# Four ring slots from the output projection to the end of cross-attention, and the first weight quad and y moved in four pieces each

## What is computed

```python
# per layer, x is the residual stream
h = rmsnorm(x, norm_mix); z, xbc, dt, q, k, v, g = split(h @ w_in)
ssd = gated_norm(ssd_scan(silu(causal_conv(xbc)), dt), z)       # 16 heads, new states are outputs
ret = gated_norm(retention(rotary(q), rotary(k), v), g)         # 4 heads, new states are outputs
x = x + concat(ssd, ret) @ w_out
x = x + cross_attend(rmsnorm(x, norm_mem), mem_k, mem_v, w_mq, w_mo)   # 4 heads, 256 memory tokens
x = x + hier_moe(rmsnorm(x, norm_ffn))                          # top group, then top 2 of 16 SwiGLU experts
# after the last layer
y = rmsnorm(x, norm_final)
```

## Time and profile before

| | us |
|---|---|
| median of three runs | 1656.1 (1656.04 to 1657.07) |
| the profiled execution's own time | 1652.09 |
| its span, first to last instruction | 1650.3 |
| TensorE busy (matmul) | 1574.4 (95% of the span) |
| VectorE busy | 548.9 (33%) |
| ScalarE busy | 291.7 (18%) |
| read from memory | 356.42 MB, 231 GB/s with the writes |

### The profile page before, as it was taken

One profiled execution on the slowest core, in us unless ns is written; L12 is line 12 of the kernel. 1 busy time (PEld: TensorE's weight loads), 2 busy tenths in 40 slices (PEclk: granted clock), 3 DMA queues, 4 the chain that ended last, 5 costly groups with the idle time before them and its releaser, 6 DMA issues.

```text
span 1650.3 us, 20355 instructions
## 1 busy us (share of the span) xinstructions
PE 1574.4 (95%) x8720; PEld 996.9 (60%) x8720; DVE 548.9 (33%) x1116; ACT 291.7 (18%) x614; POOL 14.2 (1%) x30
## 2 busy tenths in 40 slices
PE   6999999899998999999999999998999999999996
PEld 4776667677765645445377765685776665444542
DVE  1313754561132411121223066646411314121122
ACT  1003322140111201001100142212311212100102
POOL 0000000000000000000000000000000000000000
PEclk9999999999999999999999999999999999999999
DMA  6324211784257699999713241228733757999990
GB/s 271 134 102 153 87 72 52 294 318 178 103 210 299 248 378 406 394 411 411 299 58 147 102 154 56 71 110 336 276 121 142 295 207 319 409 398 412 405 394 38
DMA packets 28685, 382.48 MB, mean 232 GB/s; under 512 B 3184, under 2 KB 3568, under 8 KB 3888
## 3 DMA queue, kind: packets, MB, share of 16 engines
q1 hardware_dynamic: 25040, 356.43, 54.7%
q0 software_dynamic: 3552, 24.71, 3.7%
HBM read 356.42 MB, written 24.71 MB: 231 GB/s over the span
## 4 chain that ended last, share of the span: by engine, by line
PE 91%; DMA 4%; DVE 2%; ACT 1%; DVEq 1%; issue 1%; SPq 0%; POOL 0%; ACTq 0%; POOLq 0%
PE psum L544 38%; PE psum L1127 13%; PE psum L905 8%; PE psum L1147 7%; PE psum L1172 4%; DMA ring<-stream 4%; PE psum L1102 4%; PE psum L661 1%; PE psum L560 1%; PE psum L551 1%; PE psum L1113 1%; PE psum L984 1%; PE psum L529 1%; PE psum L752 1%; PE psum L1002 1%; PE psum L557 1%
## 5 line engine op out<-in xcount | busy, mean ns | idle before, releaser
L544 PE MATMUL psum<-h,ring 128*128 128x320 f32 x1664 | 460.8, 437 | 3.3 <-DMA ring<-stream 2.5
L544 PEld LDWEIGHTS psum<-h,ring 128*128 128x128 f32 x1664 | 316.9, 192 | 141.7 <-issue 12.0
L1127 PE MATMUL psum<-ring,work 128*64 128x512 f32 x768 | 170.7, 594 | 1.4 <-ACT work L1517 1.4
L905 PE MATMUL psum<-work,ring 128*128 128x320 f32 x512 | 139.7, 433 | 0.9 <-ACT work L1294 0.9
L544 PE MATMUL psum<-mem,ring 128*128 128x256 f32 x512 | 121.4, 393 | 6.4 <-DMA ring<-stream 6.4
L905 PEld LDWEIGHTS psum<-work,ring 128*128 128x128 f32 x512 | 96.5, 190 | 40.7 <-ACT work L1294 1.8
L1127 PEld LDWEIGHTS psum<-ring,work 128*64 128x64 f32 x768 | 53.7, 137 | 108.4 <-issue 106.6
L544 PEld LDWEIGHTS psum<-mem,ring 128*128 128x128 f32 x512 | 98.4, 196 | 27.5 <-DMA ring<-stream 7.3
L1147 PE MATMUL psum<-work 128*64 128x512 f32 x512 | 113.4, 595 | 0.7 <-ACT work L1528 0.7
L544 PE MATMUL psum<-work,ring 128*128 128x320 f32 x256 | 72.1, 444 | 14.1 <-DMA ring<-stream 13.0
L2058 DVE TENSOR_TENSOR x<-x,psum 128x320 f32<-128x320 f32 x128 | 62.5, 488 | 54.9 <-PE psum L1172 49.2
(11 more groups left out here) (284 smaller groups left out, 1369.5 us busy)
## 6 DMA issues: line engine op xcount, KB each, us to landing
ring<-stream SPq DMA_DIRECT2D x120, 2048.0 KB, 9.6
work<-stream SPq DMA_DIRECT2D x32, 2048.0 KB, 9.8
states_out<-stream SPq DMA_DIRECT2D x16, 2048.0 KB, 12.7
st_out<-states_out POOLq DMA_DIRECT2D x12, 1024.0 KB, 11.1
st_out<-work POOLq DMA_DIRECT2D x6, 1024.0 KB, 7.4
mk_out<-k_mem POOLq DMA_DIRECT2D x2, 1024.0 KB, 15.2
mv_out<-work POOLq DMA_DIRECT2D x2, 1024.0 KB, 5.7
x<-x_in SPq DMA_DIRECT2D x1, 1280.0 KB, 5.8
```

The source lines that it names most:

```text
L544: mm = pe.matmul(out, w[:, a:a + P], rhs[:, j, :], start=(j == 0), stop=(j == KD - 1))
L905: mm = pe.matmul(psum[:, j % 4, 0:T], w[:, a:a + P], src, start=(i == 0), stop=(i == 15))
L1127: mm = pe.matmul(psum[ab * CAP:(ab + 1) * CAP, up, :], h_packed[:, p % 2, k, ab * CAP:(ab + 1) * CAP], w[:, a:a + BANK], start=(k == 0), s ...
```

## The change

- `slot_of` gives q20 to q35 four slots in turn, 2, 3, 0, 1, in place of the three of the ring. The experts' six slots are taken in the order 2, 3, 0, 1, 4, 5. `use_of` counts the uses of a slot in a list of all quads.
- The waits ahead of the first load into slot 3 and into slot 4 are bound to those loads: the wait for the state stores stands ahead of q21 (before: q39), that for cross-attention and the memory values ahead of q40 as before.
- x and the parameters are issued ahead of the first constants.
- The very first quad is loaded slab by slab, with a semaphore of its own (`s_slab`) for each of the first three; the first three chunks of the first projection wait for their slab.
- y is stored by SP in four quarters, each once its two chunks are written, in place of two halves by GpSimd.

```diff
--- before.py
+++ after.py
@@ -72,18 +72,20 @@
 XT = 2 + GB
 WIDER = 6
 assert Q_MOE % RING == 0 and (QUADS - Q_MOE) % WIDER == 0
-LATER = (QUADS - Q_MOE) // WIDER
+assert (Q_MOE - Q_OUT) % 4 == 0
 
 
 def slot_of(q):
-    return q % RING if q < Q_MOE else (q - Q_MOE) % WIDER
+    if q < Q_OUT:
+        return q % RING
+    return (2, 3, 0, 1)[(q - Q_OUT) % 4] if q < Q_MOE else (2, 3, 0, 1, 4, 5)[(q - Q_MOE) % WIDER]
+
+
+SLOTS = [slot_of(q) for q in range(QUADS)]
 
 
 def use_of(L, q):
-
-    own = (Q_MOE // RING if slot_of(q) < RING else 0)
-    return L * (own + LATER) + (q // RING if q < Q_MOE else own + (q - Q_MOE) // WIDER)
-
+    return L * SLOTS.count(slot_of(q)) + SLOTS[:q].count(slot_of(q))
 
 
 XW = CW - 1 + SEQ + DB * (CW - 1 + DS)
@@ -295,6 +297,7 @@
 
         loaded = [sem(f"s_loaded{s}") for s in range(WIDER)]
         freed = [sem(f"s_freed{s}") for s in range(WIDER)]
+        s_slab = [sem(f"s_slab{i}") for i in range(3)]
         s_sq = sem("s_sq")
         s_acc = sem("s_acc")
         s_sum = sem("s_sum")
@@ -474,21 +477,27 @@
 
         @block.sync
         def _(sp):
-            sp.dma_start(cst[:, 0:FIRST], consts[:, 0:FIRST]).then_inc(s_const, 16)
             sp.dma_start(x[:], x_in).then_inc(s_const, 16)
             sp.dma_start(par[:], params.rearrange("l p n -> p l n")).then_inc(s_const, 16)
+            sp.dma_start(cst[:, 0:FIRST], consts[:, 0:FIRST]).then_inc(s_const, 16)
             for L in range(DEPTH):
                 for q in range(QUADS):
                     s, n = slot_of(q), use_of(L, q)
                     if n >= 1:
                         sp.wait_ge(freed[s], n)
-                    if q == Q_MOE + RING:
+                    if q == SLOTS.index(3):
                         for i in range(3):
                             sp.wait_ge(s_store[i], 16 * STORES[i] * (L + 1))
-                    if q == Q_MOE + RING + 1:
+                    if q == SLOTS.index(4):
                         sp.wait_ge(s_ottout, (L + 1) * 4)
                         sp.wait_ge(s_mvstore, 16 * (L + 1))
-                    sp.dma_start(slots[s], stream[L * QUADS + q]).then_inc(loaded[s], 16)
+                    if L + q == 0:
+                        for i in range(3):
+                            sp.dma_start(slots[s][:, i * SLAB:(i + 1) * SLAB], stream[q][:, i * SLAB:(i + 1) * SLAB])\
+                                .then_inc(s_slab[i], 16)
+                        sp.dma_start(slots[s][:, 3 * SLAB:], stream[q][:, 3 * SLAB:]).then_inc(loaded[s], 16)
+                    else:
+                        sp.dma_start(slots[s], stream[L * QUADS + q]).then_inc(loaded[s], 16)
                     if L == 0 and q == RING - 1:
                         sp.dma_start(cst[:, FIRST:], consts[:, FIRST:]).then_inc(s_tables, 16)
                         sp.dma_start(mem[:], mem_in).then_inc(s_mem, 16)
@@ -504,6 +513,11 @@
                                 .then_inc(d_loaded, 16)
                 with sp.Else():
                     sp.sem_inc(d_loaded, 96 * E)
+            for i in range(4):
+                c = slice(i * KD // 4, (i + 1) * KD // 4)
+                sp.wait_ge(s_h, DEPTH * KD + (i + 1) * KD // 4)
+                sp.dma_start(y_out[:, c, :], h[:, c, :]).then_inc(s_ystore, 16)
+            sp.wait_ge(s_ystore, 64)
 
 
         @block.tensor
@@ -574,7 +588,11 @@
                 def project(q0, chunks, banks=4, src=h, gained=None):
                     nonlocal n_proj
                     for c in chunks:
-                        w = quad(pe, L, q0 + c // 4)
+                        if L + q0 == 0 and c < 3:
+                            pe.wait_ge(s_slab[c], 16)
+                            w = slots[0]
+                        else:
+                            w = quad(pe, L, q0 + c // 4)
                         if n_proj >= 4:
                             evacuated(n_proj - banks)
                         products(psum[:, n_proj % banks, 0:T], w, (c % 4) * SLAB, P, src, gained).then_inc(s_proj, 1)
@@ -2173,11 +2191,6 @@
                 pool.dma_start(mk_out[L], k_mem[:]).then_inc(s_mkstore, 16)
                 pool.wait_ge(s_mkvout, L * 16 + 16)
                 pool.dma_start(mv_out[L], vt_mem[:]).then_inc(s_mvstore, 16)
-            for i in range(2):
-                c = slice(i * KD // 2, (i + 1) * KD // 2)
-                pool.wait_ge(s_h, DEPTH * KD + (i + 1) * KD // 2)
-                pool.dma_start(y_out[:, c, :], h[:, c, :]).then_inc(s_ystore, 16)
-            pool.wait_ge(s_ystore, 32)
             for i in range(3):
                 pool.wait_ge(s_store[i], 16 * STORES[i] * DEPTH)
             pool.wait_ge(s_mkstore, 16 * DEPTH)
```

## The result

The changed kernel takes **1635.3 us** (1634.8 to 1636.7) against 1656.6 us of the kernel before timed beside it (1656.0 to 1657.8): a ratio of 0.9872 with a 95% interval of 0.9855 to 0.9889, so 21.2 us less (18.4 to 24.0). Forecast were 1639.5 us and a range from 1636 to 1647.

What follows compares the result with a forecast made beforehand. TensorE was taken as the bound, losing time in waits on transfers and at its lower clock. Terms 12.1 + 3.7 + 0.8 = 16.6 us took the median of 1656.1 to 1639.5 us, range 1636 to 1647.

Steps and rivals of the forecast that it cites:

- What bounds the kernel: TensorE, busy nearly throughout, loses time in seven waits on transfers, 28.4 us in all, or at its lower clock.
- Four slots: q20 to q35: earlier loads remove cross-attention's waits for q27 and q33 and the slow clock behind q33, 12.1 us less.
- q21's wait: Ahead of the output projection: q21 now waits for all state stores, at no cost, with 13 us of cover.
- layer 1's start: First load of layer 1, delayed by the experts' new slot order: no cost, 10 us of cover.
- First quad: Kernel start: the first quarter lands at 9.2, TensorE starts at 9.3 instead of 12.96, 3.7 us less (bounds 0 and 4.6).
- y: Kernel end: four quarters from SP leave less to move after h's last column, 0.8 us less (bounds -0.5 and 1.3).
- (a): Rival at start and end: pieces pay a fixed part one after the other, gain 10.3 us, 1645.8 us; chance 7%.
- (b): Rival in cross-attention: another wait takes q33's place, half of the 12.1 us stays, 1645.5 us; chance 10%.
- (c): Rival: SP's in-order queue behind q21 passes its delay on, no load comes earlier, only 4.5 us left, 1651.6 us; 3%.
- (d): Rival, slower: the last state store lands so late that q21 holds up the output projection, 1660 us; chance 3%.
- (e): Rival, faster: two clock stretches fewer and the larger gain at the start, below 1636 us; chance 5%.
- the allowance of two stretches either way: Clock: moved work may gain or lose two stretches at 1.2 GHz behind other idle places, 3.3 us either way.

## Why the prediction missed, point by point

- **What bounds the kernel** held: TensorE's seven waits were the right place. The four in cross-attention vanished.
- **Four slots.** The mechanism held in each step: q27 and q33 took their predecessors' times, 1.8 us of cover at q33 against the 2.2 foretold, q34 in time, q21's wait free with 16 us to spare (13 foretold), layer 1's start unmoved. The size was low: 12.1 against 12.7 in the same profile and 14.1 over eight (13.2 if the 0.9 us of layer 1's new states are the slots' doing). The step that failed is reading the price of a varying wait off one execution: 34.72 and 34.24 us for the two stages of q33 stand near the short end of 34.2 to 38.1.
- **First quad.** 3.7 us were foretold; TensorE's first product starts 2.35 us earlier (12.96 to 10.61), and over the profiles with pieces and without 2.5 us earlier at a fixed point further on, the second broadcast of the decays (two matmuls of line 661 of the kernel before: 196.0 against 198.5 on average). The failing step is "a quarter of it lands 1.23 us later, at 9.2": it took the spacing of whole quads, which is that of the part that lands last, for the time of a quarter. The quarters do land 1.23 us apart and half of the first quarter is in at 9.1 us, but its last part comes at 10.5, 2.6 us behind the last part of the loads ahead of it. The bounds of 0 and 4.6 took that in.
- **y.** This term missed by most: 0.8 us foretold, 3.5 measured, outside the bounds of -0.5 and 1.3. The pieces alone are worth 0.8 us from SP. The failing step was that the 2.6 us between landing and end were taken as fixed ("the span ends about 2.6 us after y's last landing, as now"); they are the end of GpSimd's program, and with the store on SP 0.4 us are left.
- **The sum and the median.** 12.1 + 3.7 + 0.8 = 16.6 foretold; by the runs 14.1 + 2.5 + 3.5 = 20.1. Measured are 21.2 (18.4 to 24.0). The 4.0 us between profile and median were kept as if they belonged to both kernels. They were a draw: the kernel before varies over 10 us, its profiled execution was a short one, and the changed kernel's profile lies 0.5 us below its median. Adding them to the forecast of the changed kernel is the step that put 1639.5 in place of 1635.5, the forecast for a profiled execution, of which 1634.8 was measured. That this lies so close is luck in part: terms that were too small (slots and end) and losses in untouched stages made up for one another. The range allowed 3.3 us for the clock but measured it from a short execution.
- **The rivals.** (a) falls: quarters overlap, the last landing 3.7 us behind the first, and y ends sooner, not later. Its figure for the start, 2.1 us, was nearer than the forecast's 3.7, but by another mechanism. (b) falls, with 1.8 us of cover left. (c) and (d) fall on q21. (e), larger than the forecast, is what came, though from the end and from the draw rather than from an even larger start.

On the clock the prediction was right in kind: the stretch of 1.2 GHz behind q33 is gone in both layers. Other stretches come and go with the draw: between retention and new states of layer 0 the changed kernel lost 1.6 us (47.94 against 46.30), as five of the seven other profiles with three slots did or more; between new states and output projection of layer 1 it lost 1.8 (54.61 against 52.84); and ahead of the experts of layer 0 it won 1.2 (9.50 against 10.69), as some profiles with three slots do too (9.2 to 10.7). So the allowance of two stretches either way was about right, but belongs to both kernels.

## What to carry to other kernels

Before a term is read off one profile, look whether its stage has the same length in several executions; where it ends in a wait for a transfer it may not, and removing the wait is worth its average, not its reading. Look at what comes behind the last landing as well as at the landing: which engine issues the last store and waits for it can matter more than how the store is cut. When a load is cut into pieces, ask when the last part of the first piece lands, not when most of it does; two halves served here as well as four quarters.

## What the runs showed of the hardware that was not expected

- The span ended 2.6 to 2.8 us after the last landing of a store from GpSimd and 0.4 us after one from SP. Of this GpSimd's DRAIN was 2.2 to 2.35 us, SP's 0.007.
- Four queued transfers of 512 KiB in rows of 4 KB per partition moved at 269 to 297 GB/s from 7 to 9 us and at 406 to 416 from 9 to 11, where halves in rows of 8 KB and the whole quad of the kernel before, in rows of 16 KB, moved at 426 to 440 in both. The Trainium skill, DMA: Bandwidth & Descriptors, Bandwidth, asks for transfers of at least 1 MiB; here halves of exactly 1 MiB ran at the full rate from the first, quarters of 512 KiB in one queue only after their first two microseconds.
- Of the sixteen parts of the first transfer the last landed up to 1.7 us behind the fifteenth (9.32 and 11.00 us), and TensorE waits for the last.
- The granted clock fell to 1.2 GHz for most of a window of 11.5 us in which TensorE had no idle time; that cost 5.0 us in one execution, and in the one used for the prediction the same products at the same place ran at a granted clock of 1.00.
- Two executions of one kernel differed by up to 10.7 us (1650.4 to 1661.0), with mean clocks of 0.982 and 0.977.
